# A decoder block kernel on one core: the last gate columns of the attention layer as one joint seven-product projection in place of two plain products

## The reference

```python
proj = u @ w_in
q, k, v, g, fl = jnp.split(proj, [ATT_WIDTH, 2 * ATT_WIDTH, 3 * ATT_WIDTH, 4 * ATT_WIDTH], axis=-1)
...
c = jnp.cumsum(log_f, axis=1).transpose(0, 2, 1)
attn = fox_attention(heads(q), heads(k), heads(v), c)   # causal softmax, 16 heads of 64
return (attn * jax.nn.silu(g)) @ w_out
```

## Time and profile before

| | |
|---|---|
| median of 3 runs | 1992.81 us (1992.79 to 1994.95) |
| profiled execution | 1993.44 us, span 1991.6 us |
| PE busy | 1880.8 us (94%) |
| DVE, ACT, POOL busy | 790.4, 386.2, 315.9 us |
| mean granted clock of TensorE | 0.987 |
| chain that ended last | PE 55%, DMA 20%, DVE 6%, POOL 3% |

### The profile page before, as it was taken

How to read it: one execution, slowest core, us unless ns; L and a number is a source line. 1 busy time by engine, 2 the same in 40 slices (tenths; PEclk the granted TensorE clock), 3 DMA queues, 4 the chain that set the end, 5 groups by cost and what they waited for, 6 DMA issues and landing times.

```text
span 1991.6 us, 20866 instructions
## 1 busy us (share of the span) xinstructions
PE 1880.8 (94%) x8234; PEld 985.5 (49%) x8234; DVE 790.4 (40%) x1698; ACT 386.2 (19%) x753; POOL 315.9 (16%) x399
## 2 busy tenths in 40 slices
PE   8999999999999999999999999889998999989987
PEld 3678854444656544867655434334342333434333
DVE  2456676652888566568555202011110201111012
ACT  1133341204655111013310101001000100100012
POOL 2533200002788010415200000000000000000000
PEclk9999999999999999999999999999999999999999
DMA  9033331112211431221637999999999999999996
GB/s 282 16 85 85 106 127 42 43 53 94 64 43 49 177 102 52 80 44 63 238 139 295 427 427 427 427 427 428 428 427 427 428 427 428 427 428 427 428 428 266
DMA packets 101871, 488.71 MB, mean 245 GB/s; under 512 B 5903, under 2 KB 53354, under 8 KB 75792
## 3 DMA queue, kind: packets, MB, share of 16 engines
q1 hardware_dynamic: 98304, 478.69, 59.9%
q0 software_dynamic: 3184, 8.58, 1.4%
q10 hardware_dynamic: 288, 0.11, 0.0%
HBM read 485.23 MB, written 2.38 MB: 245 GB/s over the span
## 4 chain that ended last, share of the span: by engine, by line
PE 55%; DMA 20%; DVE 6%; POOL 3%; issue 1%; ACT 1%; SPq 0%; POOLq 0%; DVEq 0%; ACTq 0%
DMA arena<-in_w_up 19%; PE bank L1109 11%; PE bank L1706 9%; PE bank L1769 8%; PE bank L1079 6%; PE bank L1116 3%; PE bank L1639 3%; PE bank L1537 2%; DMA arena<-in_last_down 1%; PE bank L1754 1%; PE bank L1737 1%; PE bank L1087 1%; PE bank L1485 1%; POOL arena L943 1%; PE bank L1069 1%
## 5 line engine op out<-in xcount | busy, mean ns | idle before, releaser
L1769 PE MATMUL bank<-arena 128*64 128x512 f32 x1792 | 415.7, 620 | 68.0 <-DMA arena<-in_w_up 67.4
L1769 PEld LDWEIGHTS bank<-arena 128*64 128x64 f32 x1792 | 146.2, 142 | 336.8 <-issue 335.6
L1109 PE MATMUL bank<-arena 128*128 128x512 f32 x560 | 243.4, 593 | 0.6 <-ACT arena L1945 0.6
L3186 DVE TENSOR_TENSOR arena<-arena,bank 128x512 f32<-128x512 f32 x64 | 42.4, 685 | 475.1 <-PE bank L1665 473.8
L1079 PE MATMUL bank<-arena 128*128 128x512 f32 x416 | 182.4, 594 | 0.1
L1109 PEld LDWEIGHTS bank<-arena 128*128 128x128 f32 x560 | 105.3, 190 | 129.6 <-issue 128.2
L1053 POOL TENSOR_TENSOR small<-small 128x2 f32<-128x2 f32 x2 | 1.8, 920 | 929.0 <-DVE small L3243 929.0
L2141 ACT ACTIVATE arena<-bank,small 64x512 f32<-64x512 f32 x64 | 43.5, 682 | 522.4 <-issue 239.2
L1250 PE MATMUL bank<-arena 128*128 128x256 f32 x616 | 134.8, 380 | 0.0
L3220 DVE SCALAR_TENSOR_TENSOR arena<-bank,small,arena 64x512 f32<-64x512 f32 x64 | 47.6, 750 | 215.9 <-ACT arena L2141 213.0
L1250 PEld LDWEIGHTS bank<-arena 128*128 128x128 f32 x616 | 116.5, 190 | 18.0 <-issue 2.5
(11 more groups left out here) (371 smaller groups left out, 2254.2 us busy)
## 6 DMA issues: line engine op xcount, KB each, us to landing
arena<-in_w_down SPq DMA_DIRECT2D x60, 2048.0 KB, 26.1
arena<-in_w_gate SPq DMA_DIRECT2D x56, 2048.0 KB, 26.7
arena<-in_w_up SPq DMA_DIRECT2D x56, 2048.0 KB, 29.8
arena<-in_w_gate SPq DMA_DIRECT2D x16, 1024.0 KB, 8.0
arena<-in_w_up SPq DMA_DIRECT2D x15, 1024.0 KB, 9.7
arena<-in_att_w_in SPq DMA_DIRECT2D x24, 512.0 KB, 7.3
arena<-in_rec_w_in SPq DMA_DIRECT2D x12, 1024.0 KB, 5.5
arena<-in_ple_w_gate SPq DMA_DIRECT2D x4, 2048.0 KB, 12.6
```

Of the source, the lines that this page charges most:

```text
L1109: mm = pe.matmul(bank[:, :], x[:, k, :], w[:, k, :], start=(k == 0), stop=(k == 3))
L1769: mm = pe.matmul(banks[f][64 * part:64 * part + 64, :], xe[:, k, CAP * (e % 2):CAP * (e % 2) + CAP], w[:, kk, 512 * f:512 * f + 512], star ...
L3186: dve.tensor_tensor(H[:, i, c], H[:, i, c], moe.bank(("add", q, i, half))[:, :], ALU.add).then_inc(moe_dve, 1)
```

## The change

One entry, `("g0", 3)`, is added to `JOINTS`. The gate columns of steps 6 and 7 are thereby made together in step 6, and step 7 makes none. Since lists and waits are built from `JOINTS`, the rest of the diff only renames what transfers, sums and multiplications wait for.

```diff
-JOINTS = [("q0", 0), ("k0", 0), ("g0", 0), ("q0", 1), ("k0", 1), ("g0", 1), ("q0", 2), ("k0", 2), ("g0", 2), ("q0", 3), ("k0", 3)]
+JOINTS = [("q0", 0), ("k0", 0), ("g0", 0), ("q0", 1), ("k0", 1), ("g0", 1), ("q0", 2), ("k0", 2), ("g0", 2), ("q0", 3), ("k0", 3), ("g0", 3)]
...
-        half_slabs(("gate", 0), a["ple_w_gate"][0], (36864, 20480), (("k0", 3, "d"), ("g0s", 7)))
+        half_slabs(("gate", 0), a["ple_w_gate"][0], (36864, 20480), (("g0", 3, "d"), ("g0", 3, "d")))
...
-                        dve.wait_ge(*drained(("k0", 3, "d")))
+                        dve.wait_ge(*drained(("g0", 3, "d")))
...
-                    dve.wait_ge(gates_ready, 3 + 4 * layer + i + 1)
+                    dve.wait_ge(gates_ready, 4 + 4 * layer + i + 1)
```

## The result

| | before | after |
|---|---|---|
| median | 1994.43 us (6 runs, 1992.79 to 1995.01) | 2000.58 us (6 runs, 1998.52 to 2004.47) |
| profiled span | 1991.6 us | 1997.9 us |
| PE busy | 1880.8 us | 1877.7 us |

The ratio is 1.0038, with a 95% interval of 1.0028 to 1.0048: the change makes the kernel slower, by 5.6 to 9.6 us. Forecast were +5.4 us and 1998.2 us. Of the 2.4 us by which the median lies above that, 1.6 us lie in the kernel before, whose first three runs had a median of 1992.81 and whose six have 1994.43 us. PE is busy for 3.1 us less, and the kernel takes 6.3 us longer. In two more sets of 10 runs each the ratio was 1.0028 (1.0019 to 1.0037) and 1.0029 (1.0020 to 1.0039).

A forecast was written before the change was run, and what follows sets the result against it. The prediction took PE to bound the kernel before the experts, with attention-loop delays counting in full. It summed +4.55 us of delay and +0.85 us of clock to +5.4 us, 1992.8 to 1998.2 us, range 1996.0 to 2000.8.

The forecast's parts named there:

- What bounds the kernel: Whole kernel: PE delays before the experts also move the full transfer stream, so a microsecond in the attention loop counts in full.
- Rival 2: Expert weight stream: its start doesn't hang on PE, so the 4.55 us delay is absorbed, 1992.8 us; chance 0.10.
- The joint product is 2.1 us shorter than two plain ones: PE, steps 6 and 7: one joint gate product of 12.19 us replaces two plain ones of 14.29 us, -2.10 us.
- The sum: PE, steps 6 and 7: -2.10 fewer products, -0.50 transposes without their wait, +7.15 lost cover, together +4.55 us.
- The scores 4.55 us later, then a pause of 7.15 us: Step 7: scores start at 270.00; PE, free at 274.66, stands still until head 14 is ready at 281.81.
- Rival 3: Last pair's softmax: not needed so late, the pause fillable by the output projection's first product; -2.10 us, 1990.7 us; chance 0.05.
- What should be free: ACT's copy and table load, DVE's seven additions, POOL's four sums stay covered; a failed cover costs 0.4 to 2.9 us.
- Rival 1's second half: DVE, step 6: additions hold up the copies and so the scores, up to 2.9 us; chance 0.12 for the whole rival.
- +8.0 at most: Upper end of the rival with longer low clock or late additions: +4.55 +3.4 us, 2000.8 us; chance 0.12.
- The clock, +0.85 us: PE around the 7 us pause: clock falls, costing between nothing and 1.69 us; the middle taken, +0.85 us.
- rival 1's first half: PE around the pause: the clock stays low for longer, another 1.7 us; chance 0.12 for the whole rival.

The follow-up runs named there:

- both_early: The kernel before with both plain gate products in step 6: 2002.41 us (5 runs) against 1993.73, +8.7 us.
- no_gate7: The kernel before without the second plain gate product in step 7, so with another output: median 1998.07 us (11 runs), +4.4 us; repeated: 1994.13 us.
- weights_late: The changed kernel with DVE's two weight sums moved behind the copies of the last transposes: 1997.18 us (11 runs) against 1993.73, +3.5 us.
- early_out: The changed kernel with the output projection's first product ahead of head 14's transposes: 1993.03 us (11 runs) against 1993.65, ratio 0.9999.
- no_gate7_no_lock: no_gate7 with the range reduction of the filter's first sine kept in the PSUM bank: 1997.98 us (11 runs) against 1993.73.

## Why the prediction was right in kind and wrong in size

1. *What bounds the kernel* (a microsecond in the attention loop counts in full): right. The shift of 6.2 us at the tail is found unchanged at 1108 us, and the span is 6.3 us longer. Rival 2, absorption, is out.
2. *The joint product is 2.1 us shorter than two plain ones*: right in the sum, wrong in what it is made of. The joint product took 12.19 us, but the two plain ones take 13.84 us back to back (both_early): 1.65 us are fewer products, and 0.45 us were waits for DVE that the rows held as well. The sum goes from start to start, so its 4.55 us is not touched.
3. *The scores 4.55 us later, then a pause of 7.15 us*: right, 4.55 and 7.07. That the second product was free is shown in three profiles without it (no_gate7 and its repeats): the transposes of head 14 start 9.45 or 9.46 us after the values in all. Their medians, 4.3 and 4.4 us above the kernel before, are not explained by it. That the chain on DVE sets the pause is shown by weights_late, where 3.0 us of it went with the two sums; that the pause is the loss, by early_out, where needed work put into it brings the 6 us back. Rival 3 (the count decides) is out for the changed kernel; with the filler that it named the time is that of the kernel before within the spread, 0.8 us less in the traces and not 2.10.
4. *What should be free* was free: no wait of PE for POOL (its sums ended at 241.5), DVE's additions ahead of the copies, ACT's table loads with 0.79 us to spare. Rival 1's second half (additions hold up the scores) is out. Its "+8.0 at most" left the 2.9 us of these additions out of the sum.
5. *The clock, +0.85 us*: this step failed; it is the term of the sum that was too small. "Bounds: nothing ..., and 8.78 - 7.09 = 1.69 us" took the low stretch to be as long as behind waits of 2.6 us, and so the middle of that. The stretch was twice as long, 2.3 us in the pause and 4.6 us on work, and cost 1.64, 1.41 and 1.59 us in three profiles, 1.61 and 1.65 us in no_gate7 and its repeat, 0.9 us in no_gate7_no_lock, 2.1 us in both_early and 2.6 us in weights_late. The local price is now twice the term: 4.55 + 1.6 = 6.2 us, what the profile of the changed kernel shows. This is rival 1's first half (the clock stays low for longer) in kind, at half its price.
6. *The spread.* The first measurement, 6.15 us between its medians and +7.6 us by its ratio, lies at that or above it. The sets that followed gave +5.0 and +5.9 us, +5.6 and +5.8 by their ratios. The prediction had no term for a second level some 5 us up, which came in 5 of 26 runs, twice in the first six, and not once in 79 runs of the kernel before (1995.7 us at most). What makes it is open for the changed kernel. Seen in traces were two things that make such a level in its variants, one slow DVE instruction and a low clock on work with a second fall; which of them it is here was not caught. The mean granted clock of the five upper runs is 0.983 to 0.985, 0.9838 on average, that of the other 21 is 0.9856: by this, some 7 us more at half clock, worth 3.6 us at most if all of it lay on work. That is an estimate, and it would leave part of the 5 us to something else.

## What to carry to other kernels

Before replacing work by less work, ask what the old work covers. A product of PE that ends just when DVE has the next operands ready is a sign that one is the other's cover, and its length from start to start may hold a short wait; shortening or moving it yields a pause, and a pause of a few microseconds on PE has a price of its own in clock. If a cheaper form must stand earlier, look for the next independent work to put in its place. Times with two levels need more than six runs: compare how many runs lie in each level before reading a median.

## What the runs showed that was not expected

- After a pause of 7 us PE's clock stayed at half for 6.8 us in six profiles and for 10.2 us in both_early, in place of 3.4 us behind the wait of 2.59 us. The length of the wait alone does not decide it: behind equal waits of 3.29 us it was about 3.3 us in one profile of the kernel before and about 6.9 us in the other. A pause shortened to 4.07 us did not make it cheaper: ten records of transposes took 2.40 us in place of 1.31.
- A DVE instruction on SBUF alone (64x512, 0.42 to 0.64 us otherwise) took 6.00 us while POOL worked through a row of more than ten multiplications one after another. The Trainium skill ("SBUF — State Buffer", "Who interferes with whom") says that a `tensor_scalar` can run in a mode that takes the port pair which DVE and POOL share, and that the one that issues first then has the pair for its whole instruction while the other is fully blocked. Whether this instruction ran in that mode, no run shows. If it is this block, the trace goes further: it lasted over 11 of POOL's instructions, not one (0.45 to 0.72 us). In the kernel before the two took turns in the same place (0.61 us for DVE's, 0.63 us for POOL's beside it).
